# Preparing the first column halves of all token tiles ahead of the second halves, with the first weight pieces and x requested at once, in a hybrid linear-attention layer

## The reference

```
h    = rmsnorm(x, norm_w)
proj = h @ w_in                      # 2048 x 7184, cut into nine column ranges
o_a  = chunked_gated_linear_attention(gq, gk, gv, log_a, ...)   # 4 GLA heads
o_b  = chunked_gated_linear_attention(hq, 1 - f, hi, log f, ...) # 8 HGRN2 heads
mixed = concat(head_rmsnorm(o_a) * silu(gg), head_rmsnorm(o_b) * silu(hg))
x    = x + mixed @ w_out
return rmsnorm(x, final_norm_w)
```

## Time and profile before

| what | value |
|---|---|
| median of 3 runs | 939.58 us (939.55 to 939.67) |
| span of the profiled execution | 939.5 us (939.477 unrounded) |
| TensorE busy | 925.7 us, 99% |
| VectorE busy | 471.7 us, 50% |
| ScalarE busy | 368.3 us, 39% |
| GpSimd busy | 15.0 us, 2% |

### The profile page before, as it was taken

The page is one execution under the profiler, slowest core; times in us unless marked ns, Lnnn a source line. Parts: engine busy times, 40 slices in busy tenths (PEclk is TensorE's granted clock), DMA queues, the critical chain, the costliest instruction groups (busy, mean ns, idle before and its releaser), DMA issues.

```text
span 939.5 us, 12245 instructions
## 1 busy us (share of the span) xinstructions
PE 925.7 (99%) x4529; PEld 769.5 (82%) x4529; DVE 471.7 (50%) x788; ACT 368.3 (39%) x526; POOL 15.0 (2%) x31
## 2 busy tenths in 40 slices
PE   7999999999999999999999999999999999999996
PEld 4887888888888888888888888888888888888885
DVE  6642532227374553733576877777854442232353
ACT  6521612224252624424334544646435342322314
POOL 6000000000000000000000000000000000000000
PEclk9999999999999999999999999999999999999998
DMA  7252243332223222223322222222232355332224
GB/s 273 55 152 68 68 114 110 90 90 67 71 87 90 68 74 82 67 68 111 93 88 68 68 68 68 67 73 61 68 90 68 108 210 198 102 100 89 89 68 179
DMA packets 43858, 89.90 MB, mean 96 GB/s; under 512 B 4709, under 2 KB 4745, under 8 KB 42665
## 3 DMA queue, kind: packets, MB, share of 16 engines
q1 hardware_dynamic: 41042, 87.05, 30.8%
q10 hardware_dynamic: 2776, 2.31, 0.8%
HBM read 85.16 MB, written 4.19 MB: 95 GB/s over the span
## 4 chain that ended last, share of the span: by engine, by line
PE 97%; DVE 1%; ACT 1%; DMA 1%; issue 0%; SPq 0%; DVEq 0%; ACTq 0%
PE main L322 84%; PE sc L367 6%; PE po L391 2%; PE st L378 1%; PE po L394 1%; DVE feat L922 1%; DMA feat<-in_x 1%; PE st L356 0%; PE st L458 0%; PE st L457 0%; PE sc L437 0%; DVE w_lo L768 0%; ACT feat L600 0%; PE po L403 0%; PE sc L403 0%; PE sc L404 0%
## 5 line engine op out<-in xcount | busy, mean ns | idle before, releaser
L768 DVE TENSOR_TENSOR w_lo<-raw,w_hi 128x1024 fp32r<-128x1024 f32 x144 | 176.4, 1226 | 293.0 <-ACT w_hi L519 292.6
L519 ACT ACTIVATE w_hi<-raw 128x1024 fp32r<-128x1024 f32 x144 | 152.2, 1057 | 350.2 <-PE main L322 312.0
L322 PE MATMUL main<-h_hi,w_hi 128*128 128x512 f32 x640 | 258.3, 404 | 0.0
L322 PE MATMUL main<-h_hi,w_lo 128*128 128x512 f32 x640 | 250.4, 391 | 0.0
L322 PE MATMUL main<-h_lo,w_hi 128*128 128x512 f32 x640 | 249.3, 390 | 0.0
L322 PE MATMUL main<-w_hi,h_hi 128*128 128x512 f32 x512 | 202.7, 396 | 0.7 <-DVE h_lo L929 0.7
L322 PE MATMUL main<-w_hi,h_lo 128*128 128x512 f32 x512 | 200.7, 392 | 0.0
L322 PE MATMUL main<-w_lo,h_hi 128*128 128x512 f32 x512 | 200.3, 391 | 0.0
L322 PEld LDWEIGHTS main<-h_hi,w_lo 128*128 128x128 f32 x640 | 120.1, 188 | 26.5
L322 PEld LDWEIGHTS main<-h_hi,w_hi 128*128 128x128 f32 x640 | 120.4, 188 | 22.6
L322 PEld LDWEIGHTS main<-h_lo,w_hi 128*128 128x128 f32 x640 | 120.6, 188 | 22.3
(11 more groups left out here) (162 smaller groups left out, 607.4 us busy)
## 6 DMA issues: line engine op xcount, KB each, us to landing
raw<-in_w_in SPq DMA_DIRECT2D x112, 512.0 KB, 3.7
raw<-in_w_out SPq DMA_DIRECT2D x32, 512.0 KB, 3.7
feat<-in_x SPq DMA_DIRECT2D x6, 1024.0 KB, 7.8
val<-in_x SPq DMA_DIRECT2D x2, 1024.0 KB, 8.4
feat<-in_final_norm_w SPq DMA_DIRECT2D x1, 1024.0 KB, 9.4
out_y<-val SPq DMA_DIRECT2D x2, 512.0 KB, 2.7
out_y<-val ACTq DMA_DIRECT2D x2, 512.0 KB, 3.8
out_y<-feat SPq DMA_DIRECT2D x2, 512.0 KB, 2.7
```

Of the source, the lines that this page charges most:

```text
L322: mm = pe.matmul(main[c][:, :], a, b, start=(k == 0 and j == 0), stop=(k == KT - 1 and j == 2))
L519: act.activation(w_hi[:, q % SPL, :, :], raw[:, q % RAW, :, :], ACT.Copy).then_inc(hi_ok, 1)
L768: dve.tensor_tensor(w_lo[:, q % SPL, :, :], raw[:, q % RAW, :, :], w_hi[:, q % SPL, :, :], ALU.subtract).then_inc(lo_ok, 1)
```

## The change

Three things. (1) SP asks for the pieces 0 to 3 and the four x tiles at once: the pieces 2 and 3 land in `val`, which is not in use yet, and have semaphores of their own (`first_in`); pieces 4 and 5 follow and wait for `lo_ok` 1 and 2. (2) The order of the quarters is a table, `TURNS`: (0,0) (0,1) (0,2) (0,3) (1,0) (1,1) (2,0) (2,1) (1,2) (1,3) (3,0) (3,1) (2,2) (2,3) (3,2) (3,3), as (tile, quarter). `NORMS` gives the scalings: tile 0 in 512 + 512 + 1024 columns, the others 1024 + 1024, first halves ahead of second ones. (3) The products of the pieces 0 to 3 are interleaved with the transposes in the order of the calls of `first(tile, pieces)` below. The amount of work is the same but for one scaling of 1024 columns, which becomes two of 512.

```
+            for p in range(HP, HP + RAW):
+                sp.wait_ge(lo_ok, p % RAW + 1)
...
+            transposes((0, 0), (0, 1))
+            first(0, 0, 1)
+            transposes((0, 2), (0, 3), (1, 0), (1, 1))
+            first(1, 0, 1)
+            first(0, 2, 3)
+            first(1, 2, 3)
+            transposes((2, 0), (2, 1), (1, 2), (1, 3))
+            first(2, 0, 1, 2)
+            transposes((3, 0), (3, 1))
+            first(2, 3)
+            transposes((2, 2), (2, 3))
+            first(3, 0, 1, 2)
+            transposes((3, 2), (3, 3))
+            first(3, 3)
             pe.wait_ge(xt_lo, KT)
...
             squares(0)
-            split(0, -3)
+            split_first(0)
+            highs((0, 0))
+            split_first(1)
+            highs((0, 1))
             broadcast(2)
-            highs(0, [0])
             broadcast(3)
-            split(0, -2)
-            highs(0, [1])
             squares(1)
-            split(0, -1)
-            highs(0, [2, 3])
-            split(0, 0)
-            highs(1)
+            highs((0, 2), (0, 3), (1, 0))
+            split_first(2)
+            highs((1, 1))
+            split_first(3)
             squares(2)
...
-            highs(2)
+            highs((2, 0), (2, 1), (1, 2), (1, 3))
             squares(3)
...
-            highs(3)
+            highs((3, 0), (3, 1), (2, 2), (2, 3))
...
             act.dma_start(prow[R_HNW:R_END, 0:P], hgrn_norm_w).then_inc(par_in, 16)
+            highs((3, 2), (3, 3))
...
+            normalise(0)
+            normalise(1)
+            split_first(0)
+            lows((0, 0))
+            split_first(1)
+            lows((0, 1))
             dve.wait_ge(nb_ok_act, 2)
-            normalise(0, 1)
-            lows(0, [1])
-            normalise(1, 0)
-            normalise(1, 1)
-            split(0, -1)
-            lows(0, [2, 3])
-            split(0, 0)
-            lows(1)
...
+            normalise(2)
+            normalise(3)
+            lows((0, 2), (0, 3), (1, 0))
+            split_first(2)
+            lows((1, 1))
+            split_first(3)
+            normalise(4)
+            normalise(5)
+            lows((2, 0), (2, 1), (1, 2), (1, 3))
+            normalise(6)
+            normalise(7)
+            lows((3, 0), (3, 1), (2, 2), (2, 3))
+            normalise(8)
+            lows((3, 2), (3, 3))
```

More of the change, by code:

```diff
@@ L63 @@
 LN_SHIFT = 2
+TURNS = [(0, 0), (0, 1), (0, 2), (0, 3), (1, 0), (1, 1), (2, 0), (2, 1), (1, 2), (1, 3), (3, 0), (3, 1), (2, 2), (2, 3),
+         (3, 2), (3, 3)]
+NORMS = [(0, 0, 1), (0, 1, 2), (0, 2, 4), (1, 0, 2), (1, 2, 4), (2, 0, 2), (2, 2, 4), (3, 0, 2), (3, 2, 4)]
 G_MIN = -50.0
@@ L165, in hymba_kernel @@
         nw_in = sem("nw_in")
+        first_in = [sem(f"first_in{p}") for p in range(HP)]
         par_in = sem("par_in")
@@ L207, in wait_bank, with turn, first_raw @@
                 eng.wait_ge(piece_done, G * NP + NP)
+        def turn(t, j):
+            return TURNS.index((t, j)) + 1
+        def first_raw(p):
+            return raw[:, p, :, :] if p < RAW else val[:, p, :].rearrange("p (k n) -> p k n", k=PK)
         def ms_bank(nx):
@@ L222, in group @@
                     s = p % RAW
-                    if not (isinstance(n, int) and n < RAW):
-                        sp.wait_ge(lo_ok, n - RAW + 1)
+                    sp.wait_ge(lo_ok, n - RAW + 1)
                     rows = src[p * PK * P:(p + 1) * PK * P, bass.ds(col, GW)]
@@ L231, in x_tile, with first @@
                 sp.dma_start(xin[:, t, :], x[t * P:(t + 1) * P, :]).then_inc(x_in[t], 16)
+            def first(p):
+                rows = w_in[p * PK * P:(p + 1) * PK * P, C_GV:C_GV + GW]
+                sp.dma_start(first_raw(p), rows.rearrange("(k p) n -> p k n", p=P)).then_inc(first_in[p], 16)
             x_tile(0)
-            group(w_in, C_GV, G_V, range(0, 2))
+            first(0)
+            first(1)
             x_tile(1)
-            group(w_in, C_GV, G_V, range(2, 4))
+            first(2)
+            first(3)
             x_tile(2)
             x_tile(3)
-            group(w_in, C_GV, G_V, range(4, NP))
+            for p in range(HP, HP + RAW):
+                sp.wait_ge(lo_ok, p % RAW + 1)
+                rows = w_in[p * PK * P:(p + 1) * PK * P, C_GV:C_GV + GW]
+                sp.dma_start(raw[:, p % RAW, :, :], rows.rearrange("(k p) n -> p k n", p=P)).then_inc(raw_in[p % RAW], 16)
+            group(w_in, C_GV, G_V, range(HP + RAW, NP))
             group(w_in, C_GV + GW, G_V + 1)
@@ L339, in group, with by_tile @@
                             f()
-            def by_tile(G, pieces, before=lambda p, c: None, after=lambda p, c: None):
+            def by_tile(G, pieces):
                 for c in range(4):
@@ L346, in by_tile @@
                             pe.wait_ge(lo_ok, G * NP + (p + 1))
-                        before(p, c)
                         products(p, c, True)
-                        after(p, c)
             def head_tasks(H, X, nx, at):
@@ L428, in _, with transposes @@
             pe.wait_ge(consts, 1)
[L430 to L435, removed]
+            def transposes(*turns):
+                for t, j in turns:
+                    for n, (u, j0, j1) in enumerate(NORMS):
+                        if u == t and j0 <= j < j1:
+                            pe.wait_ge(xn_ok, n + 1)
+                    earlier = [turn(*e) for e in TURNS[:turn(t, j) - 1] if e[1] == j]
+                    if earlier:
+                        pe.wait_ge(xt_lo, earlier[-1])
                     for k in range(4 * j, 4 * j + 4):
@@ L439, in transposes, with first @@
                     mm.then_inc(xt_ps, 1)
[L441 to L451, removed]
+            def first(c, *pieces):
+                for p in pieces:
+                    pe.wait_ge(lo_ok, p + 1)
+                    if p == 0:
+                        pe.wait_ge([nb_ok, nb_ok_act][c // 2], c % 2 + 1)
+                    pe.wait_ge(xt_lo, turn(c, p // 2))
+                    products(p, c, True)
             def low_rank():
@@ L469, in decay_inputs @@
                               start=True, stop=True).then_inc(z_ps, 1)
-            transposes(0, 0)
-            by_tile(0, range(HP), before, after)
+            transposes((0, 0), (0, 1))
[12 more added lines that the diff above has]
+            first(3, 3)
             pe.wait_ge(xt_lo, KT)
@@ L509, in _, with split_first @@
             step = Steps(act, a_step)
+            def split_first(p):
+                act.wait_ge(first_in[p], 16)
+                act.activation(w_hi[:, p, :, :], first_raw(p), ACT.Copy).then_inc(hi_ok, 1)
             def split(G, p):
@@ L515, in split @@
                     return
-                act.wait_ge(raw_in[q % RAW], G * (NP // RAW * 16) + 16 * (q // RAW + 1))
-                if not (isinstance(G, int) and G * NP + q < SPL):
-                    act.wait_ge(piece_done, G * NP + (q - SPL + 1))
+                act.wait_ge(raw_in[q % RAW], G * (NP // RAW * 16) + 16 * (q // RAW + 1 - HP // RAW))
+                act.wait_ge(piece_done, G * NP + (q - SPL + 1))
                 act.activation(w_hi[:, q % SPL, :, :], raw[:, q % RAW, :, :], ACT.Copy).then_inc(hi_ok, 1)
@@ L602, in squares, with highs @@
                 act.sem_inc(xss, 1)
-            def highs(t, js=range(4)):
-                for j in js:
-                    act.wait_ge(xt_ps, 4 * t + j + 1)
+            def highs(*turns):
+                for t, j in turns:
+                    act.wait_ge(xt_ps, turn(t, j))
                     act.activation(h_hi[:, 4 * j:4 * j + 4, t * P:(t + 1) * P],
@@ L914, in _, with normalise @@
             dve.tensor_copy(ones_r[:, :], ones).then_inc(onesr_ok, 1)
-            def normalise(t, half):
-                h = slice(half * D // 2, (half + 1) * D // 2)
-                if half == 0:
+            def normalise(n):
+                t, j0, j1 = NORMS[n]
+                h = slice(j0 * 512, j1 * 512)
+                if j0 == 0:
                     dve.wait_ge(xss, t + 1)
@@ L923, in normalise, with split_first, lows @@
                                          op0=ALU.mult, op1=ALU.mult).then_inc(xn_ok, 1)
-            def lows(t, js=range(4)):
-                for j in js:
-                    dve.wait_ge(xt_hi, 4 * t + j + 1)
+            def split_first(p):
+                dve.wait_ge(hi_ok, p + 1)
+                dve.tensor_tensor(w_lo[:, p, :, :], first_raw(p), w_hi[:, p, :, :], ALU.subtract).then_inc(lo_ok, 1)
+            def lows(*turns):
+                for t, j in turns:
+                    dve.wait_ge(xt_hi, turn(t, j))
                     h = (slice(None), slice(4 * j, 4 * j + 4), slice(t * P, (t + 1) * P))
@@ L935, in _ @@
             dve.wait_ge(nb_ok, 2)
[L936 to L939, removed]
-            dve.wait_ge(nb_ok_act, 2)
-            normalise(0, 1)
-            lows(0, [1])
-            normalise(1, 0)
-            normalise(1, 1)
-            split(0, -1)
-            lows(0, [2, 3])
-            split(0, 0)
```

(6 more changed lines are left out.)

## The result

The changed kernel takes 945.75 us (median of 4 runs, 943.09 to 945.89) against 939.57 us before: ratio 1.0056, 95% interval 1.0044 to 1.0068. By the medians it is **slower by 6.2 us**. (The ratio of the medians alone would be 1.0066; the ratio given lies nearer to that of the means, 1.0059, which the one run at 943.09 us pulls down.) The prediction said slower, but by 2.8 us, with a range up to 944.6; the result lies outside. Run again beside the last experiments it gave 945.39 us (6 runs), ratio 1.0056 again.

A forecast was written before the change was run, and what follows sets the result against it. The prediction took the kernel to be as long as TensorE's work plus its losses at both ends. It summed 939.6 + 1.7 (piece 4 later) + 1.1 (slow clock) = 942.4 us, range 941.0 to 944.6.

The forecast's parts named there:

- The new wait in front of piece 4: TensorE stands still from 44.65 to 48.3 us before piece 4's first product, waiting for its split: 3.6 us.
- the 5.9 us of the forecast: Time from the last transposes (42.40 us) to piece 4's first product (48.3), through ScalarE's copies, table load and both splits.
- the requests win nothing: Transfers at the start: requesting them in advance costs nothing and wins nothing directly; VectorE and ScalarE set the pace.
- the first wait: TensorE waits 1.4 us, from 18.8 to 20.2 us, for quarter (1,0)'s `h_lo`, replacing the old 1.9 us wait.
- The table load: Rival before piece 4's ScalarE split: the load costs more than its 1.28 us row; with 1.4 more, 943.8 us; chance 0.04.
- the base of the sum: The sum starts from 939.6 us, with the profiled execution's 939.5 us span taken as within 0.1 us of the median.
- 1.9 us won up to 44.65: Gain ahead of the new wait: TensorE reaches 44.65 us where the profile before had 46.54.
- the first twelve products: Start of TensorE's work: first product at 12.3 us instead of 12.86, the 12 products end at 16.9.
- the 1.1 us that I took: Slow clock behind piece 4's wait: a loss of 1.1 us, between bounds of nothing and twice 1.6 us.
- The clock does not fall: Rival behind piece 4's wait: no clock fall, or only within the wait; 941.2 us; chance 0.16.
- The clock falls twice: Rival: clock also falls behind the 18.8 us wait, or piece 4's slow stretch is long; 944.2 us; chance 0.14.
- The faster case: Rival: the chain from the last transposes to piece 4 is hidden and 1.9 us remain won; 937.7 us; chance 0.05.

The follow-up runs named there:

- Experiment 1: Changed kernel with weight piece 4 split ahead of the copies of tile 3's last two quarters on ScalarE and VectorE: 940.11 us, ratio 1.0005.
- experiment 6: Kernel before with only tile 3's quarters 2 and 3 transposed, and copied by ScalarE, later, as in the change: 945.03 us, ratio 1.0058.
- experiment 5: Changed kernel with low-rank copy and table load moved ahead of the last two quarters' copies on ScalarE: 944.07 us, ratio 1.0036.
- experiment 4: Changed kernel with 15 unread 128x512 products added on TensorE at the start of the pause before piece 4: 943.7 us, ratio 1.0039.
- experiment 2: Kernel before with only the change's transfers, pieces 2 and 3 into `val` and all requested at once: 939.65 us, ratio 0.9999.
- experiment 8: Changed kernel, but the transfers of pieces 2 and 3 wait for the splits of pieces 0 and 1 as before: 945.79 us, ratio 1.0057.
- experiment 9: Experiment 1 plus tile 1 prepared earlier, last transposes a piece earlier, and all later scalings but one ahead of tile 2's copies: 937.95 us, ratio 0.9983.
- experiment 3: Kernel before with four more semaphores that nothing uses: 939.65 us, ratio 1.0005.

## Why the prediction was wrong

**What held.** The direction and the mechanism. The new wait in front of piece 4 was worked out as 44.65 to 48.3, 3.6 us, and measured 45.9 to 49.54, 3.6 us; the chain of ScalarE's two copies, low-rank copy, table load and split and VectorE's split took the 5.9 us of the forecast. Experiment 1 takes it away and with it 5.6 us; experiment 6 puts it alone into the old kernel and loses 5.5 us; experiment 5 shortens it and the pause follows. That the clock falls behind it was right, and experiment 4 shows that without the pause it does not. That the requests win nothing was right (experiments 2 and 8). The first product started at 12.55 for 12.3, and the first wait was 1.4 us long as said. The table load took 1.28 us and the split began 0.02 us behind it; the drain of 1.38 us that the Trainium skill ("ScalarE: Activation LUTs", what ACT_TABLE_LOAD costs) adds is not in this trace either.

**The step that failed: the base of the sum.** I wrote that "the profiled execution's span of 939.5 is within 0.1 us of the median" and counted both losses of its start, the wait and the 1.6 us of slow clock, as things a new order could win back. The device time is 1.7 to 1.8 us above the span in every run whose span is recorded; an execution with the span of that profile takes 941.1 to 941.3 us, and the median ones, at 939.58, have a span of 937.8 to 937.9 and no fall of the clock at 22.7 us. The agreement of the two numbers was a coincidence of 1.6 us of clock and 1.7 us outside the span. So the point from which the changed kernel's piece 4 had to be measured is 44.87 and not 46.54, and the "1.9 us won up to 44.65" is 0.2 us at most. This is 1.6 to 1.7 us of the 3.4 us that the forecast lacked.

**Two terms of wrong size.** I let the first twelve products reach the full clock at about 16 us, as in the earlier trace rows, and end at 16.9; in the profile of the changed kernel the half clock lasts through all twelve, to 17.8. The old order does not feel this, as experiment 2 shows, since VectorE holds TensorE back until 21.3 anyway. In the new order the transposes of the quarters (0,2) to (1,1) stand behind these products, and ScalarE and VectorE wait for them, so the first wait ended at 21.52 and not at 20.2: 1.3 us. Of these, 0.9 are the products (17.8 for 16.9), and 0.4 the first bank of transposes behind them, which takes 0.84 us (17.81 to 18.65) where it takes 0.43 at the full clock. In the profile of experiment 8 the same order reaches the full clock earlier, and the same wait ends 0.9 us earlier:

```profile
17.29 0.60 PE L462 MATMUL po<-ident,feat 128*128 128x128 f32 x4
...
20.59 0.47 PE L346 MATMUL main<-w_hi,h_hi 128*128 128x512 f32 x1 [1.39 <-DVE h_lo L974]
```

And the slow clock behind the pause cost more than the 1.1 us that I took: from 49.54 to 52.95 TensorE starts eight products in 3.4 us, where it needs 1.8 at the full clock (49.20 to 51.01 in experiment 4), a loss of 1.6 us. Nearly nothing of the slow stretch fell into the pause. So the base lacked 1.7 us, the first wait 1.2 to 1.3 and the clock 0.5, and these are the 3.4 us.

**The sum as measured.** Piece 4 starts 49.54 - 44.87 = 4.7 us later, 1.0 of it ahead of the pause (45.9 against 44.87) and 3.6 in it; with 1.6 for the clock this is 6.3, against 6.2 of the medians. The reorder had nothing to win up to 21 us: when the old kernel's wait ends at 21.26 TensorE has done twelve products and six banks of transposes, and when the new kernel's ends at 21.52 it has done the same. One wait had taken the other's place, and short ones of 0.2 to 0.4 us, for tile 2 and for tile 3's scaling, came on top; experiment 1, which has these, and one more for the last `h_lo`, but not the pause, is 0.5 us over before.

**The rivals.** "The clock does not fall" describes the run of 943.09 and that of 942.99, but with a time 1.7 us above the one I gave it. As an estimate, the span of 941.4 us of the first less the 892.9 us from piece 4 to the end puts its piece 4 at 48.5, close to the 48.3 of the forecast: what was missing there was the base alone. "The clock falls twice" did not happen at 18.8; but the slow stretch behind piece 4's wait can be a long one. The run of 946.02 us has a mean clock of 0.993, and experiment 8's profile, with 0.993 too, shows the granted clock at 0.84 in the stretch of 44.9 to 48.5 us, 0.50 to 52 and 0.68 to 55.5; from piece 4 to the end it is 944.3 - 48.58 = 895.7 us, a loss of 2.8 us and not 1.7. The faster case never showed in the changed kernel. (The 3.9 us that I gave there to four operations of ScalarE are those of five: two copies, low-rank copy, table load and split.)

What stays open: which executions see the clock fall behind a pause of 2 us, and when it rises at the start. The Trainium skill ("TensorE: Matmul & The Clock Gate", what is actually happening) says that the point at which the clock rises differs from run to run, and the traces agree: about 15.9 us in one, past 17.8 in another. That the fall behind a pause differs too is what the runs show: of the kernel before, 2 of 27 runs in one set, 1 of 17 and 2 of 17 in the others.

## What to carry to other kernels

Before a profile becomes the base of a sum, compare its span with the spans of several runs and not with the median time: a constant lies between span and time (1.7 us here), and a rare clock fall of the same size hid it. The time from a fixed point behind the change to the end of the span (892.9 us here at the full clock) tells how much of a difference lies in front of that point and how much behind it. When an order is changed so that something is prepared as late as it is needed, look at what stands behind it on the engines that prepare it: here two late copies held back the split of the next weight piece, which had been covered by 36 products and was then covered by 6. And move into an engine's idle gap only what fits into it: the fifth scaling cost 0.65 us of wait.

## What the runs showed of the hardware

The granted clock can fall behind a wait of 1.9 us and mostly does not (one profile shows it; by spans of 939.4 us and more and mean clocks of 0.995 it is 5 of 61 runs of the kernel before, and 3 of 11 with the four unused semaphores). Behind one of 3.6 us it fell in 8 of the 10 runs of the changed kernel, and in none of the 5 with the pause filled (by mean clocks of 0.996 and less against 0.998, and times of 945.3 us and more against 943.0 to 943.9).

At the start, the half clock, read from the spacing of the products, lasted until about 15.9 us (before), 16.2 (experiment 9), 16.6 (experiment 8), 17.2 (experiment 4) or beyond 17.8 (the changed kernel), in executions whose first product came at 12.54 to 12.86 us. In the new order the first wait ends with it: at 20.59 in experiment 8, 20.91 in experiment 4, 21.52 in the changed kernel. In the old order it ends at 21.25 to 21.38 in all four profiles (before, experiments 2, 3 and 6). The single runs fit this, without a profile each: experiment 1 scatters from 939.6 to 941.1 us, and the kernel before lies at 939.5 to 939.7 in 25 of 27.
